# x loaded transposed beside x, products on zeros ahead of the first tile

## The chip, the cores and the metric

The kernel runs on one core of one Trainium2 chip. The metric is the device time of one execution in microseconds; lower is better. Times inside the program are microseconds from the start of the profiled span.

## The reference

The model takes x (256 tokens, 1024 channels) through a retention layer, two PEER layers with 16384 experts, a differential attention layer, two feed-forward layers and a mixer. Only the beginning of the first layer matters here:

```python
proj = x @ w_in                      # 256x1024 @ 1024x6144
q = rope(proj[..., :hq]...)          # 4 heads of 256
k = rope(proj[..., hq:2*hq]...) * (RET_QK_DIM ** -0.5)
v, g = ...                           # 4 heads of 512 each
...                                  # per head: decayed scores, times v, norm, silu(g)
x = layer_norm(DN_ALPHA * x + mix, ln_g[l, 0], ln_b[l, 0])
```

So x is needed twice: transposed (channels on partitions) as an operand of the first products, and in its natural form (tokens on partitions) for the residual, much later.

## The kernel before

Weights stream from HBM in tiles of 128 partitions x 1024 f32 (512 KB) through a ring of six buffers (`ring`, NR = 6). SP issues the load of tile i once TensorE has "eaten" tile i - 6. Products run in fp32r, each number split in two parts: ScalarE copies a tile to `hi` (four buffers, L1008), VectorE, or for some tiles GpSimd, writes the rest, ring - hi, back into the ring's buffer as the low part (L1466, L2229). TensorE then makes three products for each chunk of 128 channels: hi x x's hi, hi x x's low, low x x's hi. For a "transposed" tile (`mat_t`, L450 to L452) these are 8 chunks x 3 = 24 products of 256 columns; for a "natural" tile (`mat_n`, L472 to L474) 12 products of 512 columns. `mat_t` waits for the low part before the first of the 24.

x itself is split alike: its transposed form `xT` has for each of 8 chunks 256 columns of hi and 256 of low. Before, SP loads the 128x128 identity and x in two halves, TensorE transposes x (L436, 16 transposes into four PSUM banks), ScalarE copies each bank to the hi columns (L1017) and VectorE subtracts for the low ones (L1443, a helper's line that most VectorE operations have).

The order on each engine is the order in which the program is written. For head 0, VectorE's is:

```python
split(tiles 0 to 3)                  # low parts
v.wait_ge(*loaded("tables"))         # rotary tables and masks, rtab
v.wait_ge(*at(mm, "ret_qk", h, z))   # tiles 0 and 1 multiplied
...                                  # the rotation of q: two products of 128x512, two sums of 128x256
split(tiles 4 and 5), then the rotation of k, then split(tiles 6 to 9)
```

Tiles 0 to 3 are ret_qk 0 to 3 (transposed form), tiles 4 to 11 are ret_vg 0 to 7 (natural form). ScalarE splits tile i + 4 only after tile i is eaten.

GpSimd issues three loads at its start, on a queue of its own: the other constants (`con`, 315 KB), the columns of gains (`col`, 44 KB) and the tables (`rtab`, 1280 KB, into `W`). Its next step is a root for head 0's norm.

Of the kernel before, what the change touches and what calls it, by code (L numbers as in the profile page):

```python
# [15 lines left out]
T = 256  # L16
DM = 1024
UNIT = 1024
NR = 6
# [10 lines left out]
SHIFT = (6, 2, 3, 0, 1, 4, 5)  # L30
ROUNDS = 14
GATE_TILE = 62

COLS = {}
_n = 0
# [117 lines left out]
def program(nc, A, out):  # L153
    ctx = ExitStack()
    with ctx:
# [3 lines left out]
        def sem(name):  # L159
            return ctx.enter_context(nc.semaphore(name))  # L160
# [69 lines left out]
        s_arrive = [sem(f"s_weight{i}") for i in range(NR)]  # L230
        s_keys = sem("s_keys")
        s_first = sem("s_first")
        s_aside = sem("s_aside")
        s_out = sem("s_out")
        load_sem = {}
# [179 lines left out]
        def tensor_program(pe):  # L415
# [13 lines left out]
            def parts(stage, src, nchunk, among=tuple(range(8)), first=0, ready=None):  # L429
                for c in range(first, nchunk, 2):  # L430
# [5 lines left out]
                            ins = pe.transpose(b[:, j * 256 + tt * 128:j * 256 + tt * 128 + 128], src(tt, c + j), ident)  # L436
                    mm.done(ins, stage, "T", c)

            def mat_t(tiles, stage, *name, among=tuple(range(8)), first=False, behind=None):

                b = bank(*name, among=among)
                for j, i in enumerate(tiles):
                    n = NTH[i] % NH
                    o = b[:, j * 256:j * 256 + 256]
                    pe.wait_ge(*low(i))
                    for k in range(8):
                        if first and j == 0 and k % 2 == 0:
                            pe.wait_ge(*at(dve, stage, "Tl", k))
                        h, l = hi[n][:, k * 128:k * 128 + 128], low_part[i % NR][:, k * 128:k * 128 + 128]
                        pe.matmul(o, h, xT[:, k, 0:256], start=k == 0, stop=False)  # L450
                        pe.matmul(o, h, xT[:, k, 256:512], start=False, stop=False)  # L451
                        ins = pe.matmul(o, l, xT[:, k, 0:256], start=False, stop=k == 7)  # L452
                    mm.done(ins, "eaten", i)
                    if j == 1:
                        mm.also(*name)
                    if behind is not None:
                        behind(j)
# [70 lines left out]
                mm.also(name, "out")  # L528

            def retention():  # L530
                pe.wait_ge(s_first, 48)
                parts("x0", lambda tt, c: tok3(x, tt, c), 8)
                q, k = R_qk
                for h in range(4):
                    for z in range(2):
                        mat_t([TILE["ret_qk", (h * 2 + z) * 2 + j] for j in range(2)], "x0", "ret_qk", h, z, first=h + z == 0)
                        if z and h:
                            pe.wait_ge(*at(dve, "ret_yn", h - 1))
                            parts(("ret", h - 1), lambda tt, c: R_yn[tt][:, c * 128:c * 128 + 128], 4)
                    for _ in mat_n([TILE["ret_vg", h * 8 + j] for j in range(4)], "x0", "ret_v", h):  # L540
                        pass
                    b = bank("ret_s", h)
                    pe.wait_ge(*at(dve, "ret_rope", h, 1))
                    for c in range(2):
                        pe.matmul(b[:, 0:256], k[:, c * 256:c * 256 + 128], q[:, c * 256:c * 256 + 256], start=c == 0, stop=c == 1)
                    for c in range(2):
                        ins = pe.matmul(b[:, 256:384], k[:, c * 256 + 128:c * 256 + 256], q[:, c * 256 + 128:c * 256 + 256],
                                        start=c == 0, stop=c == 1)
                    mm.done(ins, "ret_s", h)
                    for _ in mat_n([TILE["ret_vg", h * 8 + 4 + j] for j in range(4)], "x0", "ret_g", h):  # L550
                        pass
                    ys = [bank("ret_y", h, tt) for tt in range(2)]
                    pe.wait_ge(*at(dve, "ret_sT", h))
                    pe.wait_ge(*at(act, "ret_v", h, 1))
                    pe.matmul(ys[0], R_sT[:, 0:128], R_v[0], start=True, stop=True)
                    pe.matmul(ys[1], R_sT[:, 128:256], R_v[0], start=True, stop=False)
                    mm.done(pe.matmul(ys[1], R_sT[:, 256:384], R_v[1], start=False, stop=True), "ret_y", h)
                def last_head(k):
                    if k == 4:
                        pe.wait_ge(*at(dve, "ret_yn", 3))  # L560
                        parts(("ret", 3), lambda tt, c: R_yn[tt][:, c * 128:c * 128 + 128], 4)

                mat_out("ret_out", [TILE["ret_out", i] for i in range(16)], lambda k: R_ygT[:, k, :],
                        lambda k: [at(dve, ("ret", k // 4), "Tl", 2)] if k % 4 == 0 else [], ahead=last_head)
# [428 lines left out]
        def scalar_program(a):  # L993
# [40 lines left out]
                             "squares", stage, tt)  # L1034

            def retention():
                parts("x0", 8, xT)
                for h in range(4):
                    for z in range(2):
                        for j in range(2):  # L1040
                            split(TILE["ret_qk", (h * 2 + z) * 2 + j] + 2)
                        if z and h:
                            parts(("ret", h - 1), 4, R_ygT[:, h * 4 - 4:h * 4, :])
                    for j in range(4):
                        split(TILE["ret_vg", h * 8 + j] + 2)
                    for tt in range(2):
                        a.wait_ge(*at(mm, "ret_v", h))
                        act.done(a.activation(R_v[tt], ps("ret_v", h, tt), ACT.Copy), "ret_v", h, tt)
                        empties(act, "ret_v", h, tt)
                    for j in range(4):  # L1050
                        split(TILE["ret_vg", h * 8 + 4 + j] + 2)
                    for tt in range(2):
                        a.wait_ge(*at(mm, "ret_g", h))
                        if h:
                            a.wait_ge(*at(dve, "ret_yn", h - 1))
                        act.done(a.activation(R_sg[tt], ps("ret_g", h, tt), ACT.Silu), "ret_g", h, tt)
                        empties(act, "ret_g", h, tt)
                for i in range(16):
                    split(TILE["ret_out", i] + 2)
                    if i == 3:  # L1060
                        parts(("ret", 3), 4, R_ygT[:, 12:16, :])
# [374 lines left out]
        def vector_program(v):  # L1436
# [113 lines left out]
                empties(dve, "w_out", k)  # L1550

            def retention():
                parts("x0", 8, xT)
                for h in range(4):
                    for z in range(2):
                        for j in range(2):
# [29 lines left out]
                for i in range(15):  # L1586
                    split(TILE["ret_out", i] + 2)
                    if i == 3:
                        parts(("ret", 3), 4, R_ygT[:, 12:16, :])
                layer_norm("ret_out", 0, 0)  # L1590
                split(TILE["peer_q", 1])

# [615 lines left out]
        def gpsimd_program(p):  # L2208
# [40 lines left out]
                roots("ln", l, 1)  # L2249

            n = CONW["ident"]
            load("first", [(con[:, n:], A["con"][:, n:]), (col[:, :], A["pcol"])])
            load("tables", [(tabs, A["rtab"])])
            p.wait_ge(*loaded("first"))
# [32 lines left out]
        def sync_program(sp):  # L2287
# [4 lines left out]
                tt, half = quarter // 2, slice(quarter % 2 * 512, quarter % 2 * 512 + 512)  # L2292
                return out[tt * 128:tt * 128 + 128, half], x[:, tt, half]

            sp.dma_start(con[:, 0:n], A["con"][:, 0:n]).then_inc(s_first, 16)
            for tt in range(2):
                sp.dma_start(x[:, tt, :], A["x"][tt * 128:tt * 128 + 128, :]).then_inc(s_first, 16)
            for i, (name, idx, _) in enumerate(TILES):
                if i >= NR:
                    j = i - NR  # L2300
                    sp.wait_ge(*at(mm, "eaten", j))
                sp.dma_start(ring[i % NR][:, :], A[name][idx]).then_inc(s_arrive[i % NR], 16)
                if name == "in_fox" and idx < 4:
                    sp.wait_ge(*at(dve, "ffn", 1))
                    sp.dma_start(*aside(idx)).then_inc(s_aside, 16)
                if (name, idx) == ("w_out", 7):
                    sp.wait_ge(*at(dve, "mixed", 1))
                    for quarter in range(4):
                        sp.dma_start(*reversed(aside(quarter))).then_inc(s_aside, 16)
                if name == "peer_q" and idx % 16 == 6:  # L2310
                    l = idx // 16
                    sp.wait_ge(*at(mm, "eaten", TILE[("diff_out", 7) if l else ("ret_out", 15)]))
                    for j in range(2):
                        sp.dma_start(P_keys[:, j * UNIT:j * UNIT + UNIT], A["peer_k"][l * 2 + j]).then_inc(s_keys, 16)
# [94 lines left out]
def layout(v):  # L2409
# [49 lines left out]
    def w13(a, b):  # L2459
# [2 lines left out]

    return {
        "con": con, "rtab": rtab, "mtab": mtab, "prow": prow, "pcol": pcol, "x": v["x"][0],
        "ret_qk": np.concatenate(qk), "ret_vg": np.concatenate(vg), "ret_out": tiles_o(v["ret_w_out"][0]),
        "peer_q": np.concatenate([tiles_t(v["peer_w_q"][l]) for l in range(2)]),
        "peer_k": v["peer_subkeys"].reshape(2, 2, 8, 128, 128).transpose(0, 1, 4, 2, 3).reshape(4, 128, UNIT),
# [28 lines left out]
```

## Time and profile before

| | |
|---|---|
| median of 3 runs | 2799.11 us (2798.63, 2799.11, 2802.15) |
| profiled execution, span from first to last instruction | 2796.1 us; no other time is given for it |
| TensorE matmul busy | 2703.3 us (97%) |
| VectorE busy | 1871.7 us (67%) |
| ScalarE busy | 1254.9 us (45%) |
| GpSimd busy | 708.2 us (25%) |
| moved by DMA | 451.61 MB, mean 162 GB/s |
| mean granted TensorE clock | 0.986 |

TensorE is the engine that is busy nearly always. Its busy time is modelled from overlapping records, so the pace is better read from the starts of successive products than from their durations.

### The profile page before, as it was taken

To read this page: it belongs to the slowest core of one execution; us is meant where nothing else is said; L and a number is where in the kernel's file an instruction comes from. 1 tells how busy PE (TensorE), PEld (TensorE's weight loads), DVE (VectorE), ACT (ScalarE), POOL (GpSimd) and SP (SyncE) were. 2 spreads that over 40 slices of the span, in tenths; PEclk is the share of its full clock that TensorE was granted. 3 is DMA by queue.
4 is the path that set the end of the run, shared out by engine and by line. 5 is a ranking of instruction groups with operands and counts; after the bars stand their busy time and mean duration, and the time that the engine had idled before them with its cause. 6 is when DMAs were issued, how large, how long until landed. Compare 5 with 4: busy or idle time off the path is not lost.

```text
span 2796.1 us, 43604 instructions
## 1 busy us (share of the span) xinstructions
PE 2703.3 (97%) x17504; PEld 2453.2 (88%) x17504; DVE 1871.7 (67%) x3258; ACT 1254.9 (45%) x1774; POOL 708.2 (25%) x314
## 2 busy tenths in 40 slices
PE   8998999999999998879999999999989999999998
PEld 7888999999888886679999998888879988888997
DVE  5655898777666666757987776666665567666554
ACT  4343455333455454534463334554544465343443
POOL 0000898666000000005996662000000020000000
PEclk9999999999999999989999999999999999999999
DMA  6554555444666664335554446666645553113554
GB/s 206 166 188 159 169 180 168 141 142 138 203 194 192 194 195 141 111 131 164 180 178 142 140 140 188 192 193 194 194 146 182 189 167 130 53 61 106 164 183 158
DMA packets 124280, 451.61 MB, mean 162 GB/s; under 512 B 13856, under 2 KB 13984, under 8 KB 123952
## 3 DMA queue, kind: packets, MB, share of 16 engines
q1 hardware_dynamic: 122256, 441.57, 49.8%
q0 software_dynamic: 1824, 7.25, 0.8%
q8 instruction: 140, 2.29, 0.3%
q14 instruction: 60, 0.49, 0.1%
HBM read 446.67 MB, written 2.10 MB: 160 GB/s over the span
## 4 chain that ended last, share of the span: by engine, by line
PE 90%; DVE 5%; POOL 3%; ACT 1%; issue 1%; DMA 0%; DVEq 0%; SPq 0%; POOLq 0%; ACTq 0%
PE ps L450 13%; PE ps L451 13%; PE ps L452 13%; PE ps L485 11%; PE ps L486 11%; PE ps L487 11%; PE ps L590 4%; PE ps L472 3%; PE ps L474 3%; PE ps L473 3%; POOL ring_r L2229 2%; PE ps L715 2%; DVE W L1443 2%; DVE x L1443 1%; PE ps L436 1%
## 5 line engine op out<-in xcount | busy, mean ns | idle before, releaser
L1008 ACT ACTIVATE hi<-ring 128x1024 fp32r<-128x1024 f32 x830 | 868.6, 1052 | 403.7 <-PE ps L452 278.2
L2229 POOL TENSOR_TENSOR ring_r<-ring,hi 128x1024 fp32r<-128x1024 f32 x260 | 660.2, 2550 | 1271.9 <-ACT hi L1008 1270.8
L450 PE MATMUL ps<-xT_r,hi 128*128 128x256 f32 x3248 | 935.4, 288 | 4.9 <-DVE ring_r L1466 2.9
L451 PE MATMUL ps<-xT_r,hi 128*128 128x256 f32 x3248 | 920.6, 283 | 0.0
L452 PE MATMUL ps<-xT_r,ring_r 128*128 128x256 f32 x3248 | 920.5, 283 | 0.0
L1466 DVE TENSOR_TENSOR ring_r<-ring,hi 128x1024 fp32r<-128x1024 f32 x570 | 692.0, 1223 | 282.0 <-ACT hi L1008 281.6
L450 PEld LDWEIGHTS ps<-xT_r,hi 128*128 128x128 f32 x3248 | 625.0, 192 | 8.9 <-DVE ring_r L1466 3.3
L451 PEld LDWEIGHTS ps<-xT_r,hi 128*128 128x128 f32 x3248 | 625.4, 193 | 0.7 <-issue 0.7
L452 PEld LDWEIGHTS ps<-xT_r,ring_r 128*128 128x128 f32 x3248 | 624.5, 192 | 0.0
L485 PE MATMUL ps<-hi,oht_r 128*128 128x512 f32 x1040 | 404.9, 389 | 1.4 <-DVE ring_r L1466 1.2
L486 PE MATMUL ps<-ring_r,oht_r 128*128 128x512 f32 x1040 | 404.6, 389 | 0.0
L487 PE MATMUL ps<-hi,oht_r 128*128 128x512 f32 x1040 | 404.6, 389 | 0.0
L1088 ACT ACTIVATE oht_r<-W 128x256 fp32r<-128x256 f32 x256 | 106.7, 418 | 331.3 <-PE ps L487 331.1
L1443 DVE TENSOR_TENSOR W<-W,ps 128x512 f32<-128x512 f32 x236 | 161.8, 686 | 125.7 <-PE ps L590 105.5
L485 PEld LDWEIGHTS ps<-hi,oht_r 128*128 128x128 f32 x1040 | 195.2, 188 | 43.0 <-DVE ring_r L1466 1.8
L487 PEld LDWEIGHTS ps<-hi,oht_r 128*128 128x128 f32 x1040 | 195.2, 188 | 40.4
L486 PEld LDWEIGHTS ps<-ring_r,oht_r 128*128 128x128 f32 x1040 | 195.2, 188 | 40.2
L1686 DVE TENSOR_TENSOR oht_r<-W,oht_r 128x256 fp32r<-128x256 f32 x256 | 112.3, 439 | 133.0 <-ACT oht_r L1088 132.9
L1673 DVE TENSOR_SCALAR oht<-ps,selT 128x128 f32<-128x128 f32 x512 | 174.0, 402 | 0.0
L472 PE MATMUL ps<-hi,xT_r 128*128 128x512 f32 x336 | 135.5, 403 | 2.5 <-ACT W L1026 1.8
L590 PE MATMUL ps<-oht 128*128 128x128 f32 x1024 | 135.1, 275 | 0.0
L485 PE MATMUL ps<-hi,W_r 128*128 128x512 f32 x320 | 128.9, 403 | 5.0 <-DVE W_r L1443 4.9
(227 smaller groups left out, 2702.7 us busy)
## 6 DMA issues: line engine op xcount, KB each, us to landing
ring<-in_peer_u SPq DMA_DIRECT2D x256, 512.0 KB, 3.5
ring<-in_peer_v SPq DMA_DIRECT2D x256, 512.0 KB, 4.2
ring<-in_f SPq DMA_DIRECT2D x132, 512.0 KB, 3.5
ring<-in_ret_vg SPq DMA_DIRECT2D x32, 512.0 KB, 3.5
ring<-in_peer_q SPq DMA_DIRECT2D x32, 512.0 KB, 3.5
ring<-in_ret_qk SPq DMA_DIRECT2D x16, 512.0 KB, 3.5
ring<-in_ret_out SPq DMA_DIRECT2D x16, 512.0 KB, 3.5
ring<-in_in_shift SPq DMA_DIRECT2D x14, 512.0 KB, 3.5
```

The source lines that it names most:

```text
L450: pe.matmul(o, h, xT[:, k, 0:256], start=k == 0, stop=False)
L451: pe.matmul(o, h, xT[:, k, 256:512], start=False, stop=False)
L452: ins = pe.matmul(o, l, xT[:, k, 0:256], start=False, stop=k == 7)
L472: pe.matmul(bs[tt], xh, h, start=kk == 0, stop=False)
L485: pe.matmul(b, ah, h, start=first, stop=False)
L486: pe.matmul(b, ah, l, start=False, stop=False)
L487: return pe.matmul(b, al, h, start=False, stop=last)
L590: ins = pe.matmul(b[:, s * 128:s * 128 + 128], hot[:, s, 1, :], hot[:, s, 0, :], start=True, stop=True)
L1008: hid.done(a.activation(hi[m % NH][:, :], ring[j % NR][:, :], ACT.Copy), j)
L1443: dve.done(fn(*args), *name)
L1466: lo_v.done(v.tensor_tensor(low_part[j % NR][:, :], ring[j % NR][:, :], as32(hi[m % NH][:, :]), ALU.subtract), j)
L2229: lo_p.done(p.tensor_tensor(low_part[j % NR][:, :], ring[j % NR][:, :], as32(hi[m % NH][:, :]), ALU.subtract), j)
```

## The change

x is loaded in two forms. The transposed form `xt` (128 partitions x 8 chunks x 256 tokens), laid out before the launch, comes first on SP's queue, in four loads of two chunks (256 KB each, rows of 2 KB), into `oht`, a buffer that is otherwise first used in the PEER layer. ScalarE and VectorE split each pair from there into `xT`; the 16 transposes are gone. The identity and natural x follow later, between tiles 7 and 8. GpSimd waits for tile 1 before it issues constants, columns and tables. TensorE makes 8 products of 256 columns in plain f32 on a zeroed buffer (VectorE's memset) into PSUM bank 7. And the first tile has an order of its own: its 16 products with the hi part run once `hi` is there, the 8 with the low part after them. The order in which the partial products are added up in this tile changes with it.

```diff
+WARM = 8
...
+        s_turned = [sem(f"s_turned_x{i}") for i in range(4)]
+        x_turned = oht[:, :].rearrange("p (c t) -> p c t", c=8)
+        idle_rows = selT[:, 0:384]
...
+            def first_tile(b, i, stage):
+
+                n = NTH[i] % NH
+                o = b[:, 0:256]
+                pe.wait_ge(*at(hid, i))
+                for k in range(8):
+                    if k % 2 == 0:
+                        pe.wait_ge(*at(dve, stage, "Tl", k))
+                    h = hi[n][:, k * 128:k * 128 + 128]
+                    pe.matmul(o, h, xT[:, k, 0:256], start=k == 0, stop=False)
+                    pe.matmul(o, h, xT[:, k, 256:512], start=False, stop=False)
+                pe.wait_ge(*low(i))
+                for k in range(8):
+                    ins = pe.matmul(o, low_part[i % NR][:, k * 128:k * 128 + 128], xT[:, k, 0:256], start=False, stop=k == 7)
+                mm.done(ins, "eaten", i)
...
             def mat_t(tiles, stage, *name, among=tuple(range(8)), first=False, behind=None):
...
+                    if first and j == 0:
+                        first_tile(b, i, stage)
+                        continue
                     pe.wait_ge(*low(i))
                     for k in range(8):
-                        if first and j == 0 and k % 2 == 0:
-                            pe.wait_ge(*at(dve, stage, "Tl", k))
...
             def retention():
-                pe.wait_ge(s_first, 48)
-                parts("x0", lambda tt, c: tok3(x, tt, c), 8)
+                pe.wait_ge(*at(dve, "idle_rows"))
+                for _ in range(WARM):
+                    pe.matmul(psum[7][:, 0:256], idle_rows[:, 0:128], idle_rows[:, 128:384], start=True, stop=True)
...
                         if z and h:
+                            pe.wait_ge(s_first, 48)
...
 # ScalarE
-                parts("x0", 8, xT)
+                for c in range(0, 8, 2):
+                    a.wait_ge(s_turned[c // 2], 16)
+                    act.done(a.activation(xT[:, c:c + 2, 0:256], x_turned[:, c:c + 2, :], ACT.Copy), "x0", "Th", c)
...
 # VectorE
-                parts("x0", 8, xT)
+                step(v.memset, idle_rows, 0.0, name=("idle_rows",))
+                for c in range(0, 8, 2):
+                    v.wait_ge(*at(act, "x0", "Th", c))
+                    tt_(xT[:, c:c + 2, 256:512], x_turned[:, c:c + 2, :], as32(xT[:, c:c + 2, 0:256]), ALU.subtract,
+                        name=("x0", "Tl", c))
...
+                v.wait_ge(s_first, 48)
                 layer_norm("ret_out", 0, 0)
...
 # GpSimd
             n = CONW["ident"]
+            p.wait_ge(*arrived(1))
             load("first", [(con[:, n:], A["con"][:, n:]), (col[:, :], A["pcol"])])
             load("tables", [(tabs, A["rtab"])])
...
 # SP
-            sp.dma_start(con[:, 0:n], A["con"][:, 0:n]).then_inc(s_first, 16)
-            for tt in range(2):
-                sp.dma_start(x[:, tt, :], A["x"][tt * 128:tt * 128 + 128, :]).then_inc(s_first, 16)
+            for c in range(0, 8, 2):
+                sp.dma_start(x_turned[:, c:c + 2, :], A["xt"][:, c:c + 2, :]).then_inc(s_turned[c // 2], 16)
             for i, (name, idx, _) in enumerate(TILES):
+                if i == NR + 2:
+                    sp.dma_start(con[:, 0:n], A["con"][:, 0:n]).then_inc(s_first, 16)
+                    for tt in range(2):
+                        sp.dma_start(x[:, tt, :], A["x"][tt * 128:tt * 128 + 128, :]).then_inc(s_first, 16)
                 if i >= NR:
...
+        "xt": v["x"][0].reshape(T, 8, 128).transpose(2, 1, 0),
```

## Rows read from the trace of the kernel before

**Rows 1.** The page's chain that ended last, its shares by engine.

```profile
PE 90%; DVE 5%; POOL 3%; ACT 1%; issue 1%; DMA 0%; DVEq 0%; SPq 0%; POOLq 0%; ACTq 0%
```

**Rows 2.** TensorE's waits, whole run: us in total, times, longest us.

```profile
PE ps L436 <- DMA x<-in_x: 7.9, 1, 7.9
```

**Rows 3.** Timeline of TensorE: start us, us, engine, line, operation, out<-in, count, idle before.

```profile
7.86 3.67 PE L436 MATMUL ps<-con,x 128*128 128x128 f32 x16 [7.86 <-DMA x<-in_x]
...
14.42 0.58 PE L450 MATMUL ps<-xT_r,hi 128*128 128x256 f32 x1 [2.89 <-DVE ring_r L1466]
...
28.41 0.40 PE L472 MATMUL ps<-hi,xT_r 128*128 128x512 f32 x1
...
39.32 1.02 PE L545 MATMUL ps<-W 128*128 128x256 f32 x4
```

**Rows 4.** Timeline of ScalarE, the first 15 us.

```profile
12.06 2.06 ACT L1008 ACTIVATE hi<-ring 128x1024 fp32r<-128x1024 f32 x2
14.33 1.06 ACT L1008 ACTIVATE hi<-ring 128x1024 fp32r<-128x1024 f32 x1 [0.21 <-DMA ring<-in_ret_qk]
```

**Rows 5.** Timeline of VectorE, 13 to 28 us.

```profile
13.14 4.80 DVE L1466 TENSOR_TENSOR ring_r<-ring,hi 128x1024 fp32r<-128x1024 f32 x4 [0.25 <-ACT hi L1008]
22.91 1.42 DVE L1443 TENSOR_TENSOR W<-ps,W 128x512 f32<-128x512 f32 x2 [4.97 <-PE ps L452]
...
25.17 2.35 DVE L1466 TENSOR_TENSOR ring_r<-ring,hi 128x1024 fp32r<-128x1024 f32 x2
```

**Rows 6.** Timeline of the DMA issues and of GpSimd.

```profile
1.19 0.90 SPq L2297 DMA_DIRECT2D x<-in_x  x2
1.27 0.70 POOL L2217 DMA_DIRECT2D con<-in_con  x1 [0.82 <-POOLq L2489]
...
2.13 2.30 SPq L2302 DMA_DIRECT2D ring<-in_ret_qk  x4
2.50 0.53 POOL L2217 DMA_DIRECT2D W<-in_rtab  x1
...
56.56 1.55 POOL L2236 TENSOR_TENSOR W<-W,con 128x2 f32<-128x2 f32 x1 [53.53 <-DVE W L1443]
```

**Rows 7.** DMA issues in short stretches: KB each, median us from issue to landing.

```profile
con<-in_con POOLq DMA_DIRECT2D x1, 315.0 KB, 5.2
...
x<-in_x SPq DMA_DIRECT2D x1, 512.0 KB, 6.2
...
ring<-in_ret_qk SPq DMA_DIRECT2D x1, 512.0 KB, 9.4
...
W<-in_rtab POOLq DMA_DIRECT2D x1, 1280.0 KB, 9.6
...
ring<-in_ret_vg SPq DMA_DIRECT2D x1, 512.0 KB, 3.4
```

**Rows 8.** Windows: stretch, busy by engine, PEclk, DMA share, GB/s.

```profile
2.00:3.00 1.00, 0.00 (x0) 0.00 (x0) 0.00 (x0) 0.02 (x1) 1.00 (x2) 1.00 0.86 141
3.00:4.00 1.00, 0.00 (x0) 0.00 (x0) 0.00 (x0) 0.00 (x0) 0.04 (x1) 1.00 0.95 347
...
11.00:12.00 1.00, 0.53 (x3) 0.13 (x1) 0.84 (x2) 0.74 (x2) 0.00 (x0) 1.00 1.01 412
...
14.42:19.75 5.33, 5.33 (x25) 5.33 (x26) 3.45 (x3) 2.03 (x2) 0.00 (x0) 1.00 0.53 209
19.75:28.58 8.83, 8.83 (x74) 8.83 (x74) 4.51 (x6) 3.19 (x3) 0.00 (x0) 1.00 0.56 179
```

**Rows 9.** DMA issues late in the run, as rows 7.

```profile
selT<-in_mtab POOLq DMA_DIRECT2D x1, 352.0 KB, 3.5
...
xT<-in_prow POOLq DMA_DIRECT2D x1, 512.0 KB, 4.4
```

**Rows 10.** A late pause of TensorE: the timeline, and the window behind it.

```profile
2569.41 0.56 PE L485 MATMUL ps<-hi,W_r 128*128 128x512 f32 x1 [1.92 <-DVE W_r L1443]
...
2569.70:2573.00 3.30, 3.30 (x9) 2.59 (x8) 3.30 (x5) 0.36 (x1) 0.00 (x0) 0.50 0.15 57
```

## The prediction

> **What bounds the kernel now.** I read the chain of waits first. TensorE holds nine tenths of it [rows 1], so time saved elsewhere counts only where TensorE stands still. Then I read TensorE's own waits, the longest totals first: its only wait for a transfer is 7.9 us for x at the start [rows 2]; in the timeline, 2.89 us for the first tile's low part follow [rows 3]. The change touches only the start, so the rest is read from the timeline of the first 30 us.
>
> - TensorE transposes x from 7.86 to 11.53, starts the first product at 14.42, and starts the fifth tile (ret_vg 0, the first of the "natural" form) at 28.41 [rows 3]. In that stretch nothing else stops it, so 28.41 is the mark against which I measure: whatever the change takes off that time comes off the end, as long as the same work follows at the same pace.
> - From 14.42 to 19.75 there are 25 products of 256 columns in 5.33 us, 0.213 each, and from 19.75 to 28.58 there are 74 in 8.83, 0.119 each [rows 8]. 256 columns in 0.213 us is the 1.2 GHz level, and the later pace goes with 2.4 GHz. A tile of 24 products takes 2.87 us at the fast level. The first tile took about 5.3 us, so the slow level cost about 2.5. In this stretch the engine never paused, and then it rose. The granted clock reads 1.00 in both windows, also in the slow one [rows 8], so here I go by the pace.
> - ScalarE and VectorE split x chunk pair by chunk pair behind the transposes, and only then turn to the weight tiles: the first two hi copies end at 14.12, and the four low parts take 4.80 us from 13.14, 1.2 each [rows 4, 5]. Only tile 2 was waited for as a transfer [rows 4].
>
> **The change part by part.**
>
> *Transfers on SP's queue.* Removed from the front: the identity (64 KB) and natural x (2 x 512 KB). Added: four loads of 256 KB. The bytes are nearly the same (1.05 against 1.11 MB). Four issues at about 0.43 us replace three [rows 6], so tile 0 is issued at about 2.5 instead of 2.13. But GpSimd's three loads no longer compete. Before, the second half of x landed at 1.6 + 6.2 = 7.8 and tile 0 at 2.13 + 9.4 = 11.5 [rows 6, 7]: 524 KB in 3.7 us is 142 GB/s, while all queues together moved about 412 [rows 8]. The other 270 were GpSimd's. The queue alone should move 350 to 412 GB/s. From 2 to 3.5 us all queues moved 0.31 MB (141 + half of 347) [rows 8]; x is now issued 0.44 us earlier without the 64 KB before it, so I take 0.28 MB moved by 3.1. The other 0.77 MB take 2.0 us, and landing is told about 0.5 us after the last byte (a lone tile lands 3.4 us after its issue, of which 1.3 are transfer [rows 7]). Estimate: x landed at 5.6, tile 0 at 6.9, tile 1 at 8.1 (524 KB at 412 GB/s are 1.27 us a tile). No load in rows of 2 KB is in this stretch. The nearest is GpSimd's 352 KB in rows of 2.8 KB, which landed after 3.5 us where 512 KB in rows of 4 KB take 3.4 [rows 7, 9]: at worst the price of a byte is 1.5 times as high, and x lands 1.3 us later. At best it is nothing, and shorter rows excluding a gain, I take 0.1 us.
>
> *Split of x.* Four ScalarE copies and four VectorE subtractions of 128x512 stay, now from SBUF instead of PSUM. From SBUF, 128x1024 take ScalarE 1.03 and VectorE 1.2; VectorE's 128x512 with a PSUM operand takes 0.71 [rows 4, 5]. So I take 0.6 and 0.7 each. They run as the pairs land and end at about 6.3 and 7.0, beside the arrival of tile 0, so they cost nothing. If all four landed together, they would end at 8.4 and cost about 1 us. VectorE's memset of 384 columns is under 0.5 us, long before its first split at about 4, and costs nothing.
>
> *Transposes.* 16 records, 3.67 us, go [rows 3]; they lay entirely on the path.
>
> *First tile.* It still has 24 products, but the 16 of the high part wait only for the hi copy: 6.85 + 1.06 = 7.9, so TensorE starts at 8.0. The low part (1.22 us) ends at 9.2, while the 16 products last until 9.9; it is covered. Tiles 1 to 3 arrive at 8.1, 9.4 and 10.7 and need 2.5 us for hi and low, so they too are ready before TensorE reaches them at 10.9, 13.7 and 16.6. TensorE would be through tile 3 at 8.0 + 4 x 2.87 = 19.5. By this alone the gain is 28.41 - 19.5 = 8.9 us.
>
> *Products on zeros.* Eight plain f32 products of 256 columns. The two plain f32 products of L545 leave four records, so each makes two passes over its columns [rows 3]; by the pace above, a product is then 0.86 us at the slow level and 0.43 at the fast one. From about 1.3 they last until 4.7 if all are fast and 8.2 if all are slow; x and tile 0 hide them up to 8.0, so they can cost 0.3 us at most. What they may give is the fast level from the first product, which I counted above. Against it, between 7.86 and 14.42 the engine did 3.67 us of transposes and did not rise [rows 3]. If zeros don't raise it either, tiles 0 to 3 end at 22.0 instead of 19.5.
>
> Of this the Trainium skill, TensorE: Matmul & The Clock Gate, Part 4: PE-mode transpose, says that transpose mode does not count as busy in the way products do. The trace agrees in so far as 3.67 us of transposes brought no rise. By that rule the added products, being no transposes, would count, and the tiles would end at 19.5.
>
> *Constants and tables.* This is the part that I think decides. GpSimd now waits for tile 1 (8.1) before it issues 315, 44 and 1280 KB. Behind that wait stand only its own later steps, the first of which is at 56.56, so nothing on GpSimd is late [rows 6]. But VectorE needs the rotary tables after it has made the low part of tile 3, and the low part of tile 4 is queued behind that rotation. Before, GpSimd's issues began at 1.27, and rtab landed at 2.50 + 9.6 = 12.1: 10.8 us for all three, with SP's queue full all the time [rows 6, 7]. Now SP's queue is again full while they flow: tiles 4 and 5 are still out, tile 6 is released at 10.9, tile 7 at 13.7, and the identity and natural x (1.11 MB) come straight behind tile 7. So the tables land at 8.1 + 10.8 = 18.9. Lower bound: GpSimd's 352 KB load landed after 3.5 us [rows 9], so a fixed 2.6 us, plus 1.68 MB at 412 GB/s (4.1), gives 14.8. Upper bound: everything on SP's queue up to natural x goes first, 8.0 MB in all: 0.28 by 3.1, the rest at 0.41 MB per us, plus 0.5, is 22.5. I take 18.4, near the first row, since that has the same three loads under the same competition, less 0.5 us because a GpSimd load of 512 KB later landed in 4.4 [rows 9], where the first one here took 5.2 for 315 KB [rows 7].
>
> From the tables on, VectorE repeats what it did from 22.91: four rotation steps and the low part of tile 4, which ended 25.17 + 1.2 = 26.4, so 3.5 us [rows 5]. TensorE starts tile 4 at 18.4 + 3.6 = 22.0, 2.5 us after it ran dry. Gain at the mark: 28.41 - 22.0 = 6.4 us. Behind it, tile 6 needs its low part after tile 5's low part, the second rotation (2.3) and its own 1.2: 22.0 + 4.7 = 26.7, while TensorE comes to it at 22.0 + 2 x 2.87 = 27.7 (a natural tile streams the same columns). It holds.
>
> *What the new pause costs in clock.* Late in the run TensorE paused 1.92 us, and the next 3.3 us were granted 0.50 [rows 10]: half of that is 1.7 us lost. One such row doesn't say that every pause of 2.5 us does it. Bounds 0 and 1.7; I take 0.9.
>
> *Natural x later.* VectorE's new wait for it stands ahead of the layer norm behind ret_out, near 210 us; TensorE's is ahead of the transposes of head 0, near 65 us, which wait for VectorE anyway. Both land by about 23. Tile 8 stands behind it on SP's queue, would land at about 24 and is needed after tile 4 + 4 x 2.87 = 33. It costs nothing.
>
> Sum: 6.4 - 0.9 = 5.5 us. The profiled span is 2796.1; the profile gives no other time of that execution, and the median of the runs is 3.0 above the span. Taken off the median: 2799.1 - 5.5 = 2793.6.
>
> **The rivals.**
>
> *B, the tables are hidden.* If they land before 19.5 - 3.6 = 15.9, TensorE never runs dry and the gain is 8.9: 2790.2. For it: the lower bound of 14.8. Against it: 142 GB/s is what a queue kept beside GpSimd's, so SP's tiles take a share too.
>
> The Trainium skill, DMA: Bandwidth & Descriptors, Anatomy of one DMA, gives a GpSimd load about 2.0 us plus its bytes at 436 GB/s; by it rtab would take 5.0 us from its issue at 9.3 and land at 14.3, which is this rival. The 9.6 us of the same load here disagree with it, under competition.
>
> *C, SP's queue goes first.* Tables at 22.5, tile 4 at 26.1, gain 2.3, less a clock loss of 0.9: 2797.7. For it: before, tile 0 was late behind GpSimd's loads, so whichever queue is favoured delays the other by microseconds. Against it: then it was GpSimd's that was favoured.
>
> *D, zeros don't raise the clock.* Tiles end at 22.0, when tile 4 is just ready: the tables cover the loss and the pause is gone. Gain 6.4, at most 0.5 less: 2793. By the time alone it can't be told from the forecast, so I count it inside.
>
> *E, slower: the tables starve.* Place: GpSimd's loads against SP's queue, which now never drains, since each eaten tile refills it and natural x is added. It decides from the point where the tables land after 28.41 - 3.6 = 24.8. From 9.7 on, that is 1.68 MB in 14.6 us, under 115 GB/s. At half of the 142 that a minority queue kept, 71 GB/s, they need 23.7 us, land at 33.9, and tile 4 starts at 37.5: 9.1 us later than before, 2808.2. Against it: rtab kept two thirds of the rate, not one.
>
> **How the numbers follow.** Forecast (with D) 0.66, B 0.17, C 0.12, E 0.05. The forecast's own spread is about 2.5 us: tables 17.8 to 19.4, clock 0 to 1.7. The three runs differ by 3.5 us by themselves. Within the range of 2789.5 to 2797.5 lie the forecast, B, and a part of C. A change of 0.2% is 5.6 us, about what a measurement of this kernel can tell from none; that is 2793.5, in the middle of my forecast. So faster takes B and 0.47 of the forecast (0.48), same takes the rest with C (0.47), slower is E (0.05).
>
> **What would show it.** TensorE's first product at about 8, at 0.12 us a product (the zeros raised the clock) or 0.21 (D). A wait of TensorE on a low part (L1466) of 1 to 4 us before the first L472, with VectorE idle until the rtab load lands near 18.4; no such wait would be B. Rtab's time to landing: 9 us as before, or 5. A stretch at 0.50 right behind the pause. The forecast is wrong if tile 0 lands past 9 because rows of 2 KB are slow, or if the first L472 is not near 22.

## The result, and the profile after

The changed kernel takes 2803.66 us (median of 20 runs, 2801.41 to 2805.66), and before takes 2800.04 (20 runs). The ratio is 1.0013, 95% interval 1.0007 to 1.0019. It is 3.6 us slower, where I had forecast 5.5 us faster. The profiled execution has a span of 2800.2 us against 2796.1. One later run, of e1, took 3204.52 us at a mean granted clock of 0.785, in a state that no other run was in, and stays out of every ratio.

The head gained nearly what I said, though not for the reasons I gave. First TensorE's timeline (start us, duration, line, operation, count, idle before).

```profile
1.33 6.26 PE L554 MATMUL ps<-selT 128*128 128x256 f32 x16 [1.33 <-DVE selT L1468]
9.64 0.39 PE L452 MATMUL ps<-xT_r,hi 128*128 128x256 f32 x1 [2.05 <-ACT hi L1031]
...
23.05 0.50 PE L493 MATMUL ps<-hi,xT_r 128*128 128x512 f32 x1
```

The first product starts at 9.64 instead of 14.42, and tile 4 at 23.05 instead of 28.41 [rows 3]: 5.36 us gained at the mark. GpSimd's root for each head's norm is a marker that shows how far the gain goes. The last head's, in the changed kernel and then before:

```profile
166.26 1.60 POOL L2266 TENSOR_TENSOR W<-W,con 128x2 f32<-128x2 f32 x1 [36.73 <-DVE W L1468]
```

```profile
171.54 1.60 POOL L2236 TENSOR_TENSOR W<-W,con 128x2 f32<-128x2 f32 x1 [36.73 <-DVE W L1443]
```

The first head's root starts at 51.30, against 56.56 [rows 6]. So the gain is 5.3 us at the first head and still 5.3 at the last. All that is lost is lost in stages whose text the diff seems not to touch. TensorE's waits over the whole run (us in total, times, longest) name two that before does not have.

```profile
PE ps L506 <- DVE W L1468: 3.0, 2, 1.6
PE ps L452 <- DVE xT_r L1468: 2.5, 7, 0.8
```

The first is a wait ahead of each PEER layer's first peer_v product. Here it is in the changed kernel, and then the same place before, where the products run on without a pause.

```profile
704.09 0.50 PE L506 MATMUL ps<-hi,oht_r 128*128 128x512 f32 x1 [1.40 <-DVE W L1468]
```

```profile
708.51 0.40 PE L485 MATMUL ps<-hi,oht_r 128*128 128x512 f32 x1
```

**Theory 1, banks.** TensorE's program takes a PSUM bank for each result from a rotation over eight (`turn`, `bank`). The removed transposes took four turns. So every later result in that rotation lies four banks further on, though its code is the same. Written out from the program, peer_v 0 took bank 0 before, last held by the gate product 61; now it takes bank 4, last held by the last peer_u pair (126), whose GELU and gate have just begun. TensorE has to wait for them.

**Theory 3, the later first tiles.** (I came to it only after e7 and e8.) `first_tile` is called wherever `mat_t` has `first=True`: for x, and also in both PEER layers, both feed-forward layers and the mixer. There the low part has long been ready. The old order gave TensorE three products for each chunk as x's parts arrived; the new one gives it two and keeps eight for the end. The waits on `xT_r` (L452, 2.5 us in 7) are that. Their longest, 0.8 us ahead of the mixer's first tile, needs both faults: it is absent where either one is undone (e1, e10).

**Theory 2** is the rival to both: the loss is chance or the clock's own rhythm, moved by the earlier start.

### The profile page after: what moved, and what is told of

Its sections match the earlier page's. It is cut to its first block, busy times and chain, and to the rows that moved or that the text cites. A ratio compares the mean times of both kernels' runs of the same rounds, so it can differ in the third digit from the quotient of the medians.

```text
span 2800.2 us, 43607 instructions
## 1 busy us (share of the span) xinstructions
PE 2708.9 (97%) x17504; PEld 2457.0 (88%) x17504; DVE 1872.3 (67%) x3259; ACT 1255.2 (45%) x1774; POOL 708.3 (25%) x314
## 4 chain that ended last, share of the span: by engine, by line
PE 89%; DVE 5%; POOL 3%; ACT 1%; issue 1%; DMA 1%; SPq 0%; DVEq 0%; POOLq 0%; ACTq 0%
PE ps L471 13%; PE ps L472 13%; PE ps L473 13%; PE ps L506 11%; PE ps L508 11%; PE ps L507 10%; PE ps L613 4%; PE ps L493 3%; PE ps L495 3%; PE ps L494 2%; POOL ring_r L2259 2%; DVE W L1468 2%; PE ps L738 2%; DVE x L1468 1%; PE ps L440 1%
## 5 line engine op out<-in xcount | busy, mean ns | idle before, releaser
L471 PE MATMUL ps<-xT_r,hi 128*128 128x256 f32 x3200 | 918.9, 287 | 1.5 <-POOL ring_r L2259 1.5
L473 PE MATMUL ps<-xT_r,ring_r 128*128 128x256 f32 x3200 | 905.8, 283 | 0.0
L472 PE MATMUL ps<-xT_r,hi 128*128 128x256 f32 x3200 | 905.7, 283 | 0.0
L471 PEld LDWEIGHTS ps<-xT_r,hi 128*128 128x128 f32 x3200 | 614.1, 192 | 3.7 <-issue 2.0
L472 PEld LDWEIGHTS ps<-xT_r,hi 128*128 128x128 f32 x3200 | 614.6, 192 | 0.7 <-issue 0.7
L473 PEld LDWEIGHTS ps<-xT_r,ring_r 128*128 128x128 f32 x3200 | 613.9, 192 | 0.0
```

## The experiments

All are timed in 5 rounds against before on the same chip. Each ratio is followed by its 95% interval.

### e1_banks and e2_before_banks: the rotation

```diff
-            turn = {}
+            turn = {tuple(range(8)): 4}
```

> The changed kernel, with the one difference that the rotation over all eight PSUM banks begins at bank 4 (turn = {tuple(range(8)): 4}), so that every later product lands in the bank that it had before the change. Theory 1 (the removed transposes took four turns of the rotation, and the shift by four costs the PEER, diff and mixer stages new waits for banks): the 1.4 and 1.6 us waits ahead of the two peer_v groups and the 0.75 us one at 2264 go, and the time is 5 to 6 us under before, about 2794.5. Theory 2 (the loss behind the head comes from the start having moved against the clock's own rhythm, or from chance): the waits stay or others come, and the time stays at 2803 to 2804.

> The kernel before, with nothing changed but the rotation over all eight PSUM banks begun at bank 4. Theory 1 (the shift by four is what costs): about 6 to 9 us slower than before, 2806 to 2809, with a wait of 1.4 us ahead of the first peer_v product that before does not have. Theory 2 (the shift costs nothing; it is the start that moved): 2800, as before.

Measured: e1_banks 2798.48 us, ratio 0.9994 (0.9984 to 1.0003); e2_before_banks 2804.02, ratio 1.0014 (1.0005 to 1.0023). One line takes 5.2 us off the changed kernel and puts 3.9 us on the kernel before. In e2_before_banks the wait stands where theory 1 puts it:

```profile
709.51 0.50 PE L485 MATMUL ps<-hi,oht_r 128*128 128x512 f32 x1 [1.40 <-DVE W L1443]
```

So theory 1 is shown, in both directions. In e2_before_banks's profile the places of the two waits lose 1.7 and 1.8 us against before, 3.5 of the 3.9. But e1_banks was to give 5 to 6 us under before and gave 1.7, and e2_before_banks was to be 6 to 9 slower and was 3.9. The sizes were off, and something else was open.

### e3_banks_tables and e4_banks_zeros12: the head again

```diff
# e3: on top of e1
-            load("first", [(con[:, n:], A["con"][:, n:]), (col[:, :], A["pcol"])])
             load("tables", [(tabs, A["rtab"])])
+            load("first", [(con[:, n:], A["con"][:, n:]), (col[:, :], A["pcol"])])
# e4: on top of e1
-WARM = 8
+WARM = 12
```

> As e1_banks, and GpSimd issues the rotary tables ahead of the constants and columns. If the tables set the start of tile 4 (23.05 in the changed kernel, 0.4 us after TensorE ran dry), they now land about 2 us sooner and tile 4 starts at 22.7, a gain of only 0.3 to 0.4 us over e1_banks, since TensorE itself is then the bound. If the tables cost more than that one wait (the rival), the gain is 2 us.

> As e1_banks, with 12 products on zeros instead of 8, which fill TensorE's pause from 7.6 to 9.6 us. If the pause is what dropped the clock at 9.91, the first tile now runs at 0.12 us a product, tile 3 is through 1.6 us sooner (21.1), but tile 4 waits for the tables until 23.0 all the same: 0 to 0.3 us gain over e1_banks. The rival, that the tables don't bind, gives 1.6 us.

Measured: e3 2798.1, 0.9994 (0.9985 to 1.0003), 0.4 us under e1, as forecast and within the noise; its tile 4 starts at 22.85, e1's at 23.37. e4 2800.48, 1.0002 (0.9993 to 1.0011), by the medians 2 us worse than e1, which neither theory had, though the two intervals overlap. The start of tile 4 in e4's timeline of TensorE, and its windows (length, then busy us and count of PE, its weight loads, DVE, ACT and POOL, as in rows 8; the granted clock is third from the end) show what filling the pause did to the head.

```profile
23.55 0.72 PE L493 MATMUL ps<-hi,xT_r 128*128 128x512 f32 x1 [2.10 <-DVE ring_r L1491]
```

```profile
9.67:21.40 11.73, 11.73 (x96) 11.57 (x96) 6.23 (x6) 5.83 (x6) 1.77 (x3) 1.00 1.03 412
23.70:27.10 3.40, 3.40 (x9) 2.66 (x10) 3.30 (x6) 0.00 (x0) 0.00 (x0) 0.50 0.60 240
```

Here the clock stays up and the 96 products of tiles 0 to 3 take 11.73 us. Then TensorE stands 2.10 us ahead of tile 4, for the tables, and the clock falls there instead. The faster head bought a pause and a slow stretch of 3.4 us. In the changed kernel it was the other way round: the clock fell at the first tile, and the tables were then hidden but for 0.15 us. e1_banks, with the changed kernel's eight products on zeros, shows e4's case in its profile (a pause of 1.92 us and 0.50 from 24.4 to 27.8), so the changed kernel's head can go either way. For the same reason the head does not explain why e4's median lies 2 us above e1's. That stays open.

### e5_before_again and e6_before_delay: does a shift reach the end?

```diff
# e6: the kernel before
                 parts("x0", lambda tt, c: tok3(x, tt, c), 8)
+                for _ in range(19):
+                    pe.matmul(psum[7][:, 0:256], x[:, 0, 0:128], x[:, 0, 128:384], start=True, stop=True)
```

> The kernel before, unchanged, for a second profile of it: it shows how much of the differences behind the head are chance of the clock. If the profile of before that I read was an ordinary one, this one has the same stretches at half clock (the 6.8 us one near 1167, none near 2310 or between 2440 and 2480). If it was a lucky one, there are one or two more, 1.7 us each. Time 2800.

> The kernel before with 19 plain f32 products on x behind the transposes, nothing else: the first tile starts near 22.4 instead of 14.4, but at the fast clock, so that tile 4 starts about 5.5 us later, near 33.9. If a shift of the head goes through to the end (theory A), the time is 2805.5. If the stages behind it take up part of any shift (theory B, which would explain why e1_banks and e3_banks_tables give 2 us of the 3 to 5 that their heads gained), it is 2802 to 2803.

Measured: e5 2800.2, 1.0001 (0.9992 to 1.001); e6 2802.98, 1.0011 (1.0002 to 1.002). By the medians, 3.0 us slower, it is what theory B had. But the shift was smaller than the 5.5 that both theories started from: e6 starts tile 4 at 32.73, 4.32 us after the 28.41 of before. Its span is 2800.4 against 2796.1, again 4.3.

```profile
32.73 0.40 PE L472 MATMUL ps<-hi,xT_r 128*128 128x512 f32 x1
```

I laid the starts of TensorE's instructions side by side. From there on the two executions agree, in sum over each stage, within 0.1 us. So the later stages hand a shift on when the clock falls in the same places. e5 says how far chance goes: near 1060 it has 10.2 us at half clock where the first profile has 6.8, near 1141 it has 3.4 more, and from tile 4 on it takes 2.5 us longer. Its profiled run is at the median (2800.32); the first profile of before is of a faster execution, which is why e6 is 4.3 us behind it in span and 3.0 behind the median.

### e7_banks_full_head and e8_banks_no_zeros

```diff
# e7: on top of e3
-WARM = 8
+WARM = 12
-            p.wait_ge(*arrived(1))
+            p.wait_ge(*arrived(0))
# e8: on top of e1
-WARM = 8
+WARM = 0
```

> The changed kernel with the banks set right, 12 products on zeros, and GpSimd waiting only for tile 0 and issuing the tables first. The tables should land near 17.2, before tile 3 is through (21.2), so TensorE pauses neither before the first tile nor before tile 4, and the clock falls in neither place. Tile 4 starts at 21.3: 7.1 us before the kernel before. By theory A the time is 2793, by theory B 2796. The rival that the tables' bytes now push tile 2 back (it has 3 us to spare) would show as a wait on L1491's low part of tile 2 and a start of tile 4 past 22.

> The changed kernel with the banks set right and without the products on zeros. The first tile then starts at 9.7 at 0.21 us a product and stays slow for 3.4 to 6.8 us. Tile 4 starts at 23.2 to 24.5, against 23.0 to 23.4 with them, and without a pause ahead of it, so the clock doesn't fall there. The zeros are worth between -1 and +1 us: 2798.4 within 1 us. If they are worth the 2.5 us that I gave them, it is 2801.

Measured: e7 2797.1, 0.9989 (0.998 to 0.9998), above both theories; e8 2799.87, 0.9998 (0.9989 to 1.0007). e7's head is as expected, with no slow product and only 0.26 us of pause before the first tile, and tile 4 starts at 21.23. The window of its first tiles:

```profile
9.30:21.20 11.90, 11.70 (x96) 11.57 (x96) 8.30 (x10) 5.45 (x6) 1.15 (x3) 1.00 1.02 411
```

That is 7.2 us gained at the mark, and 2.9 at the end. e8 starts its first tile at 10.76 in its profile, not at 9.7, because the transfers landed later, and tile 4 at 24.78; the zeros are worth 1.4 us by the medians, at the edge of what these runs tell apart. The five variants with banks set right (e1, e3, e4, e7, e8) now all came out 3.4 to 5.2 us behind the gain at their marks. Chance would hardly do that five times. Set side by side with e6, each was longer by 1.9 to 2.4 us outside the slow stretches, always in the same places: the first tiles of the second PEER layer, of both feed-forward layers and of the mixer, and one pause near 1134 (0.35). That brought theory 3.

### e9 to e12: first_tile for x alone

```diff
# e9 on e7, e10 on the changed kernel, e11 on e1
-                    if first and j == 0:
+                    if first and j == 0 and stage == "x0":
                         first_tile(b, i, stage)
                         continue
                     pe.wait_ge(*low(i))
                     for k in range(8):
+                        if first and j == 0 and k % 2 == 0:
+                            pe.wait_ge(*at(dve, stage, "Tl", k))
# e12: the kernel before, first_tile where stage != "x0"
```

> As e7_banks_full_head, and first_tile is used for the stage x0 alone; the first tiles of the five later stages (two PEER, two feed-forward, the mixer) keep the order that they had before. Theory 3: the new order costs those stages about 0.5 us each, because TensorE waits for the last chunk pairs with nothing but high products to do, where before the low ones filled the wait; behind the points at which the clock's rhythm locks, this grows to 3 us. Then the head's 6.5 to 7 us come through: 2793.5. Rival: those waits are taken up by the clock windows, and the loss behind the head has another cause: 2796.5 to 2797, as e7.

> The changed kernel with first_tile for stage x0 alone, banks still shifted. Theory 3 with theory 1: 2803.7 - 3 = 2800.5. If only the banks matter: 2803.7.

> The changed kernel with the banks set right and first_tile for stage x0 alone: everything as the change meant it, with none of its two side effects. It should give what the head gives by itself, 3.3 to 5.3 us (the second where the clock falls at 9.9 and not at 24): 2795.5. If it stays at e1_banks's 2798.4, theory 3 falls.

> The kernel before with the new order of products (high parts first) in the first tiles of the five later stages only; the head and the banks are as before. Theory 3: 2 to 3.5 us slower, 2802 to 2803.5. Rival: 2800.

| | us | ratio to before | interval |
|---|---|---|---|
| e9, best head, both set right | 2794.13 | 0.9978 | 0.9969 to 0.9987 |
| e10, the change, first_tile for x alone | 2798.99 | 0.9995 | 0.9986 to 1.0004 |
| e11, the change, both set right | 2795.95 | 0.9987 | 0.9978 to 0.9996 |
| e12, before, first_tile in the later stages | 2802.86 | 1.0012 | 1.0003 to 1.0021 |

All four came within about 1.5 us of theory 3. e12 has the waits and none of the change (L448 is its `first_tile`):

```profile
PE ps L448 <- DVE xT_r L1462: 2.2, 6, 0.4
```

e11 has no wait on `xT_r` in any later stage and none on W ahead of peer_v. From 2060 us on, e9's and e11's traces run with before's, stage for stage, within 0.1 us. Ahead of that they lose 2.4 and 1.7 us from the mark on, mostly in the same two places, near 1060 and 1141, where e5, which is before again, loses its 2.5.

What the order costs can be read at the tiles themselves. From the first product of a first tile to the product behind its last, in us:

| first tile of | before | e12 | e9 | e7 |
|---|---|---|---|---|
| second PEER layer | 2.97 | 3.28 | 3.00 | 3.24 |
| first feed-forward layer | 3.90 | 4.62 | 3.90 | 4.62 |
| mixer | 4.05 | 4.62 | 4.05 | 4.62 |
| second feed-forward layer | 4.05 | 4.61 | 4.05 | 4.62 |

These four lose 2.2 us in e12 and 2.1 in e7. (The first PEER layer's tile lies partly in a slow stretch in each of these executions and can't be compared. Slow stretches touch three of these four too, by up to 1.8 us, so the split between waits and clock is rough.) The price at the end was 3.0 us (e7 to e9), 4.7 (after to e10), 2.5 (e1 to e11) and 2.9 (before to e12). So in e7 and e12 most of it is at the tiles, and the rest is where the clock falls. These two windows are the same part of the mixer, in the changed kernel and then before.

```profile
2455.00:2480.00 25.00, 24.88 (x145) 21.12 (x144) 13.02 (x21) 6.75 (x14) 0.00 (x0) 0.86 0.10 35
```

```profile
2450.00:2476.00 26.00, 25.88 (x172) 21.71 (x171) 15.98 (x26) 9.19 (x19) 0.00 (x0) 1.00 0.14 42
```

The changed kernel has two stretches at half clock in it (mean 0.86), and before has none. e10 and e12 have two as well, and so has e2, which has the shifted banks alone; e9, e11, e5 and e6 have none, nor has e1, which still has the new order. That looks like a loss of some 3 us, but the windows are too narrow. Before has its slow stretches on either side, 6.8 us from 2395.6 and 3.4 from 2569.6, where the changed kernel has 3.4 and none. The whole part, 1218 products, first in the changed kernel and then before, differs by 0.4 us, at the same mean clock:

```profile
2393.00:2593.40 200.40, 191.53 (x1218) 166.60 (x1217) 123.07 (x204) 75.64 (x133) 6.42 (x5) 0.97 0.24 75
```

```profile
2390.00:2590.00 200.00, 191.55 (x1218) 165.89 (x1217) 123.20 (x204) 75.69 (x133) 6.42 (x5) 0.97 0.23 75
```

A slow stretch that before lacks and nothing makes up for is this one of the changed kernel, which costs 1.5 us:

```profile
2310.50:2313.90 3.40, 3.40 (x19) 3.40 (x18) 3.37 (x5) 0.27 (x1) 0.00 (x0) 0.50 0.43 170
```

e1, e4 and e8 have it too; e10, e7 and e12 do not, so it goes with neither fault as such. In the profiles the changed kernel loses 9.4 us on before from tile 4 on: 3.5 at the two peer_v, 3.5 at the four first tiles (0.75 of it the wait that needs both faults), 1.5 in this stretch, 0.4 in the mixer's part above, and some 0.6 in small pieces. How the clock's share would average over many starts, I have not tested.

## Why the prediction was wrong

**What the change touches: this step failed.** I wrote that "the change touches only the start", and took 28.41 as the mark on the condition that "the same work follows at the same pace". It doesn't, twice over. For the transposes I counted 3.67 us and not the four turns of the bank rotation that went with them: 3.9 us (e2) to 5.2 (after to e1). For the first tile I followed `first_tile` in one stage; its condition holds in six. That is 2.5 to 4.7 us, of which 2.1 to 2.2 are at the tiles themselves in e7 and e12. Together with the head's gain this gives the result: after to e11, which undoes both, is 7.7 us. With both undone, the change is 0.9987 of before, 4.1 us faster.

**The sum for the head was about right, by luck: errors that cancelled.** I had 6.4 us at the mark and 0.9 lost to the clock behind it, 5.5 in all. Measured were 5.36 at the mark and, in this execution, no slow stretch behind it, since the clock had fallen at the first tile instead. Tile 0's hi copy began at 8.53 and tile 1's at 9.89, not 6.9 and 8.2. I had put the stretch's rate at 350 to 412 GB/s from 3.1 on; it was less.

```profile
3.00:4.00 1.00, 1.00 (x3) 0.78 (x3) 0.00 (x0) 0.00 (x0) 0.00 (x0) 1.00 0.79 244
...
6.00:7.00 1.00, 1.00 (x5) 0.82 (x5) 0.88 (x2) 0.94 (x2) 0.00 (x0) 1.00 0.99 346
```

From 3 to 4 us before had 347 [rows 8]. Tile 0 came 1.6 us late, past even my worst case of 1.3 us for the 2 KB rows, where I had taken 0.1. That the rows' size did it is not shown: from 6 to 7, when nearly all packets were already tile 0's of 4 KB, the rate was still 346, and no run varies the rows. Against this, the tables took less than I gave them, 9.3 us from GpSimd's first issue, at 10.16, to the landing of rtab at 19.5, where I had 10.3 (8.1 to 18.4). rtab itself landed after 8.1 us, not 9.6. SP's queue had run dry by 14 and left it nearly alone until 17. GpSimd's timeline of the changed kernel, then its DMA issues of 1 to 14 us.

```profile
10.16 0.70 POOL L2247 DMA_DIRECT2D con<-in_con  x1 [9.71 <-DMA ring<-in_ret_qk]
...
11.39 0.56 POOL L2247 DMA_DIRECT2D W<-in_rtab  x1
```

```profile
W<-in_rtab POOLq DMA_DIRECT2D x1, 1280.0 KB, 8.1
```

The bytes of tiles 4 and 5 had gone by the time that rtab's flowed, since GpSimd started late.

**The tables decide when tile 4 starts: right in kind.** VectorE's rotation began at 19.52, when they landed, and tile 4 started 3.53 us behind, as the 3.6 of the sum. I expected a pause of 2.5 us there; in this execution it was 0.15, since the first tile came late and ran slow. e1 and e4 show the pause, 1.9 and 2.1 us, with the fall of the clock behind it that I had priced at 0 to 1.7.

**Zeros.** They raised the clock. In e1, e4 and e7 the first tile runs at the fast pace, and in e8, without them, it starts at 0.21 us a product. I placed them as hiding the wait until 8.0; they ended at 7.6, the tile came at 9.6, and in the profiled execution the clock fell again at 9.9.

```profile
10.00:11.00 1.00, 1.00 (x7) 1.00 (x6) 0.87 (x2) 0.94 (x1) 0.84 (x2) 0.50 1.04 426
```

That pause I had not foreseen, because I had tile 0 too early. Its length does not decide alone: with eight products the pause was 1.7 to 2.8 us, and the clock fell in after, e3 and e11 (2.05, 2.63, 2.84) and not in e1 and e10 (1.68, 2.66). With twelve it was 0.3 to 1.1 us, and the clock fell in none of e4, e7 and e9. The Trainium skill, TensorE: Matmul & The Clock Gate, Part 4: PE-mode transpose, says that transpose mode does not count as busy in the way that other products do. The traces agree: 3.67 us of transposes raised nothing [rows 3, 8], and plain f32 products, even on zeros, did, 16 records in 6.26 us.

**The rivals.** None was right. E, the slower one, was about the tables starving, and they did not. My slower case was a mishap in the head, where I had looked closely, and not one in the stages that I had not looked at.

## What to carry to other kernels

Before costing an edit as local, list what it shares with the rest of the program: counters and rotations that later code reads (here PSUM banks), and every call that meets the condition of a new branch. If both are right and a shift still doesn't reach the end, lay the two traces side by side by instruction and sum the differences by stage, inside and outside the slow stretches apart. Small differences outside them, in the same places in every variant, are the cause to look for. Before calling a slow stretch a loss, look at the stretches beside it: the same work can be slow in other places for nearly the same sum. And when one wait in a chain is shortened, price the pause that forms behind it together with the clock: filling the first gap alone (e4) gained nothing, and moving the tables up as well (e7, e9) made the kernel faster. e9 is the best version here, 5.9 us under before.

## What the runs showed of the hardware

TensorE's slow stretches fell on the same products in executions that were shifted against each other as a whole: e6 started tile 4 4.3 us later than before and e9 5.8 us earlier, and in the mixer both had them where before has them. Kernels with a few tenths of a microsecond more between two pauses (e7, e8, e12) had them in other places there, 6.8 and 3.4 us in the one pattern and three times 3.4 in the other, and the part took 200.0 us in the one and 200.3 to 200.5 in the other.

Two queues that were both full moved nearly the same number of packets, so the one with the longer rows got more bytes. These are GpSimd's queue, with rtab in rows of 10 KB, and SP's, with tiles in rows of 4 KB, in the kernel before from 7 to 10 us (packets, MB, share of the 16 engines).

```profile
q0 software_dynamic: 91, 0.93, 73.0%
q1 hardware_dynamic: 94, 0.34, 28.0%
```

And one pause near 1134 us is 0.35 us longer in every kernel with the new head, e9 and e11 included, with the same banks and the same order of work. In e9 VectorE waits 0.46 us for a product shortly before it (1129.05), which it does not in before. Its cause is open.
